# The low part of a weight piece in two halves in the delta-rule sections of a two-block transformer kernel

## The chip, the cores and the metric

The kernel runs on one core of one Trainium2 chip. The metric is device time in microseconds; lower is better. Before the change it is 1813.97 us, the median of three runs (1813.86, 1813.97 and 1814.95).

## The reference, cut to what matters

Two blocks of two layers each, on 256 tokens of width 1024, in float32. All weights are float32 and every projection is a dense product of the 256 rows with a weight matrix. In the second block a layer computes, among others, a gated delta rule over 8 heads:

```python
proj = h @ w_in                       # many sections of 1024 columns
(dn_q, dn_k, dn_v, dn_z, dn_b, dn_a, sw_q, sw_k, sw_v, gate_a, gate_b) = split(proj)
L = where(strict, einsum('id,jd->ij', k * beta, k) * decay, 0)
u = triangular_solve(L, v * beta)     # per head and chunk: (I + L)^-1
w = triangular_solve(L, k * beta * exp(g))
# then a scan over the chunks with a 128x128 state for each head
y_a = deltanet(...) @ w_up_dn
y_b = window_attention(...) @ w_up_sw
mix = (sigmoid(gate_a) * y_a + sigmoid(gate_b) * y_b) @ w_o
```

The triangular solves are done as an explicit inverse by doubling: seven levels, each a pair of small products that depend on the level before.

## The kernel before, in words

**Dense products.** Each float32 product is made of three products in the fast float32r format: the weight is cut into a high part `hi` and a remainder `lo`, the activations into `xh` and `xl`, and TensorE adds `xh*hi`, `xh*lo` and `xl*hi` (lines 400, 401 and 402, in `multiply`). A weight unit of 128 x 2048 values comes by one DMA from SyncE's queue into one of 4 buffers `raw` (`load_unit`). It is worked in two *pieces* of 128 x 1024. For each piece ScalarE copies `raw` to `hi` (line 372, `split_hi`, a ring of 6) and VectorE subtracts `raw - hi` into `lo` (line 382, `split_lo`, a ring of 5). A piece holds two row blocks of the weight (`kk` = 0 in the left 512 columns, 1 in the right 512), and TensorE does 12 matmuls of 128x512 on it: two row blocks by two token blocks by three terms. There are 504 pieces; 496 are 128x1024 and 8 are 128x544. TensorE waits on the semaphore `lo_ready` once for each call of `multiply`, for the whole piece. VectorE makes `lo` three pieces ahead of TensorE (`LO_LEAD`).

**The order of the work** is a list of steps written out by hand (`plan_one`, `plan_two`). Each engine runs through the same list and does its own share of each step, in order. `("piece", g)` is a piece of dense work. Between the pieces stand small steps: attention, transposes (`turn`), the delta rule. What an engine does at a step waits on semaphores of the engines that feed it, and everything behind it on that engine waits too.

**The delta-rule sections.** In each layer of the second block, the sections `gb`, `ga`, `zz` and `us` (32 pieces) are run with `halves=True`: TensorE does the first row block of a piece at `("piece", g, "half")`, then one slot of small steps, then the second row block at `("more", g)`, then another slot. So there are 64 slots. An even slot stands behind a first half, an odd one behind a second half:

```python
self.steps.append(("piece", g, "half"))
if between: self.steps.extend(between.pop(0))
self.steps.append(("more", g))
```

VectorE calls `split_lo` at `piece` for a whole piece of 128x1024 and does nothing for the dense work at `more`.

The delta rule works on four pairs of heads, `g` = 0 to 3. For each pair the steps `rows`, `betas`, `gram`, `gram_q`, `mask`/`join` and `inverse` prepare the matrices, then the levels follow, alternately `level_y` in an even slot and `level_t` in an odd slot. These are the lines that the prediction speaks of:

- L1601, TensorE at `level_y`: waits for the `inverse` of the level before and for a mask from POOL (L2214). L1617 and L1620, TensorE at `level_t`; L2111, VectorE at `level_t`: subtracts the result, which the next L1601 waits for.
- L1581, TensorE at `inverse` (an odd slot): waits for VectorE's L2105, which waits for POOL's mask L2205 and stands in VectorE's order behind `gram_q` (L2099, four instructions, the even slot before) for pairs 1 to 3. For pair 0 `gram` is in slot 3 (L2090), `gram_q` in slot 4 (L2099), and `inverse` in slot 7.
- L1983, VectorE at `squares_turn` (an odd slot, in pair 0's levels): copies 16 sums, from which POOL makes a reciprocal root (L924, L930). POOL's next mask (L2214) stands behind that. The convolution of `dv` (L1934, L1936, eight instructions) is VectorE's work of the even slot before.
- L1952 and L2122 are further VectorE steps in odd slots (a transposed copy, and the state of the delta rule).

Of the kernel before, what the change touches and what calls it, by code (L numbers as in the profile page):

```python
# [17 lines left out]
F32 = mybir.dt.float32  # L18
F32R = mybir.dt.float32r
I32 = mybir.dt.int32  # L20
ALU = mybir.AluOpType
# [16 lines left out]
RAW = 4  # L38
HI_RING = 6
LO_RING = 5  # L40
LEAD = 4
LO_LEAD = 3
# [225 lines left out]
class Core:  # L268
# [74 lines left out]
    def load_unit(self, sp, u):  # L343

        job, n, layer = self.units[u]
        if u >= RAW:
            sp.wait_ge(self.lo_ready, 2 * (u - RAW) + 2)
        slot, k = u % RAW, job.unit
        r0 = (job.row + n * k) * P
        src = self.ins[job.weight][layer, r0:r0 + k * P, job.col:job.col + job.cols].rearrange("(k p) c -> p k c", p=P)  # L350
        dst = self.raw[slot][:, 0:k * job.cols].rearrange("p (k c) -> p k c", k=k)
        if u == 0:
            sp.dma_start(dst[:, 0:k // 2, :], src[:, 0:k // 2, :]).then_inc(self.first_loaded, 16)
            dst, src = dst[:, k // 2:, :], src[:, k // 2:, :]
        sp.dma_start(dst, src).then_inc(self.unit_loaded[slot], 16)
# [16 lines left out]
            act.activation(self.hi[g % HI_RING][:, 0:w], src, ACT.Copy).then_inc(self.hi_ready, 1)  # L372
            self.hi_at = g + 1

    def split_lo(self, dve, upto):

        for g in range(self.lo_at, min(upto, len(self.pieces))):
            src, w = self.piece_raw(g)
            dve.wait_ge(self.hi_ready, g + 1)
            if g >= LO_RING:  # L380
                dve.wait_ge(self.pieces_used, g - LO_RING + 1)
            dve.tensor_tensor(self.lo[g % LO_RING][:, 0:w], src, self.hi[g % HI_RING][:, 0:w].bitcast(F32),  # L382
                              ALU.subtract).then_inc(self.lo_ready, 1)
            self.lo_at = g + 1

    def multiply(self, pe, g, rows=(0, 1), blocks=(0, 1)):


        job, n = self.pieces[g]
        pe.wait_ge(self.lo_ready, g + 1)  # L390
        k, c, slot = job.unit // 2, job.cols, g
        xh, xl = self.xh[job.xt], self.xl[job.xt]
        for kk in rows[:k]:
            row = job.xt_block + n * k + kk
            w = slice(kk * c, kk * c + c)
            for tb in blocks:
                out, t = self.bank[job.banks[tb]][:, 0:c], slice(tb * P, tb * P + P)
                first = job.start and n == 0 and kk == 0
                last = job.stop and n == job.pieces - 1 and kk == k - 1
                pe.matmul(out, xh[:, row, t], self.hi[slot % HI_RING][:, w], start=first, stop=False)  # L400
                pe.matmul(out, xh[:, row, t], self.lo[slot % LO_RING][:, w], start=False, stop=False)  # L401
                mm = pe.matmul(out, xl[:, row, t], self.hi[slot % HI_RING][:, w], start=False, stop=last)  # L402
        if rows[-1] >= k - 1 and blocks[-1] == TB - 1:
            mm.then_inc(self.pieces_used, 1)
        return mm
# [888 lines left out]
def block_two(nc, core, s, plans, ins):  # L1294
# [61 lines left out]
    parts = [(0, slice(0, P), own), (1, slice(P, 3 * P), both)]  # L1356
# [496 lines left out]
    def _(dve):  # L1853
        for plan in plans:
            layer, base = plan.layer, plan.base
            for what in plan.all_steps(s):
                kind, arg = what[0], what[1] if len(what) > 1 else None
                if kind in ("piece", "second"):
                    core.split_lo(dve, base + arg + LO_LEAD + 1)
                if kind == "first":  # L1860
                    core.split_lo(dve, base + min(arg + LO_LEAD + 1, what[2] + LO_RING))
                if kind == "x_final":
# [9 lines left out]
                if kind == "post_y":  # L1872
                    c, tb = what[2:]
                    cols = slice(c * CH, c * CH + CH)
# [13 lines left out]
                if kind == "turn_rows":  # L1888
                    tb, half = what[2:]
                    for j in range(4):  # L1890
                        n = 4 * half + j
# [8 lines left out]
                if kind == "turn":  # L1900
                    f = what[2]
                    bank = B[core.turn_bank[s.stage, arg, f]][:, :].rearrange("p (j t) -> p j t", j=2)
                    if is_cut(arg):
                        if arg[0] == "f":
                            k = 4 * (int(arg[1:]) % 2) + 2 * f
# [6 lines left out]
                        if arg == "yd":  # L1912
                            for j in range(2):
                                n = 2 * f + j
# [7 lines left out]
                    elif arg in conv_out:  # L1922
# [3 lines left out]
                        for j in (3, 2, 1, 0):  # L1926
                            if j < 3:
                                dve.wait_ge(*at("taps", (arg, f, j + 1)))
                            for n in range(2):
                                w = t.cols_all[:, layer, tap(j, first + 2 * f + n):tap(j, first + 2 * f + n) + 1]  # L1930
# [64 lines left out]
                if kind == "evac":  # L1995
                    job, name = plan.by_name[arg], arg[:2]
                    c = int(arg[-1])
                    cols = slice(c * CH, c * CH + CH)
# [107 lines left out]
                if kind == "level_t":  # L2106
                    g, l = arg, what[2]
# [199 lines left out]
```

## Time and profile before

| what | value |
|---|---|
| median of three runs | 1813.97 us |
| profiled execution, its own time | 1814.69 us |
| its span | 1812.9 us |
| TensorE busy | 1764.5 us, 97% |
| VectorE busy | 1148.3 us, 63% |
| ScalarE busy | 911.5 us, 50% |
| GpSimd (POOL) busy | 212.2 us, 12% |
| `lo` pieces (L382) | 504, 605.6 us in all |
| granted TensorE clock | 0.996 of full |

Times are of one profiled execution. The engines are called PE (TensorE), PEld (its weight loads), DVE (VectorE), ACT (ScalarE), POOL (GpSimd) and SP (SyncE). A matmul's record starts when it is issued and overlaps the next one, so the distance from start to start is what one costs. The same holds for short distances on DVE: an instruction may start a little before the one ahead of it has ended. "Idle before" is the time for which the engine had nothing running, and the arrow names what ended it; an engine with no idle time shown went on without a break.

### The profile page before, as it was taken

To read this page: it belongs to the slowest core of one execution; us is meant where nothing else is said; L and a number is where in the kernel's file an instruction comes from. 1 tells how busy PE (TensorE), PEld (TensorE's weight loads), DVE (VectorE), ACT (ScalarE), POOL (GpSimd) and SP (SyncE) were. 2 spreads that over 40 slices of the span, in tenths; PEclk is the share of its full clock that TensorE was granted. 3 is DMA by queue.
4 is the path that set the end of the run, shared out by engine and by line. 5 is a ranking of instruction groups with operands and counts; after the bars stand their busy time and mean duration, and the time that the engine had idled before them with its cause. 6 is when DMAs were issued, how large, how long until landed. Compare 5 with 4: busy or idle time off the path is not lost.

```text
span 1812.9 us, 27874 instructions
## 1 busy us (share of the span) xinstructions
PE 1764.5 (97%) x10637; PEld 1441.4 (80%) x10637; DVE 1148.3 (63%) x2136; ACT 911.5 (50%) x1646; POOL 212.2 (12%) x354
## 2 busy tenths in 40 slices
PE   9999999999999999999999999999999899999998
PEld 7878888887887788777787778888877787778887
DVE  5656667765666676687555675556587655675554
ACT  5355474543545646575444454446576334455443
POOL 2203000031030000301102000000301211100000
PEclk9999999999999999999999999999999999999999
DMA  8544445554444455432222555554533222445552
GB/s 302 170 136 142 159 140 166 186 178 171 140 140 159 137 176 193 162 117 94 75 89 81 174 163 187 186 186 147 199 120 101 70 90 71 163 159 176 184 185 87
DMA packets 137131, 270.07 MB, mean 149 GB/s; under 512 B 5548, under 2 KB 8744, under 8 KB 137000
## 3 DMA queue, kind: packets, MB, share of 16 engines
q1 hardware_dynamic: 134928, 265.44, 43.9%
q10 hardware_dynamic: 2072, 2.86, 0.5%
q8 instruction: 86, 1.41, 0.3%
q14 instruction: 45, 0.37, 0.1%
HBM read 267.23 MB, written 1.05 MB: 148 GB/s over the span
## 4 chain that ended last, share of the span: by engine, by line
PE 86%; DVE 6%; ACT 3%; POOL 3%; issue 2%; DMA 0%; ACTq 0%; DVEq 0%; POOLq 0%
PE bank L400 23%; PE bank L402 23%; PE bank L401 22%; PE bank L424 4%; PE bank L1601 1%; DVE buf L1936 1%; PE bank L1617 1%; DVE lo L382 1%; PE bank L1620 1%; POOL scratch L944 1%; POOL small L930 1%; PE bank L586 1%; PE bank L1572 1%; ACT hi L372 1%; DVE buf L1934 0%
## 5 line engine op out<-in xcount | busy, mean ns | idle before, releaser
L400 PE MATMUL bank<-hi,xh 128*128 128x512 f32 (+1 forms) x2016 | 816.8, 405 | 6.4 <-issue 2.9
L402 PE MATMUL bank<-hi,xl 128*128 128x512 f32 (+1 forms) x2016 | 787.0, 390 | 0.0
L401 PE MATMUL bank<-lo,xh 128*128 128x512 f32 (+1 forms) x2016 | 784.6, 389 | 0.0
L382 DVE TENSOR_TENSOR lo<-raw,hi 128x1024 fp32r<-128x1024 f32 (+1 forms) x504 | 605.6, 1220 | 52.8 <-PE bank L402 39.4
L372 ACT ACTIVATE hi<-raw 128x1024 fp32r<-128x1024 f32 (+1 forms) x504 | 519.5, 1048 | 208.2 <-PE bank L402 207.7
L400 PEld LDWEIGHTS bank<-hi,xh 128*128 128x128 f32 x2016 | 379.8, 188 | 86.9 <-issue 14.8
L402 PEld LDWEIGHTS bank<-hi,xl 128*128 128x128 f32 x2016 | 379.1, 188 | 81.7
L401 PEld LDWEIGHTS bank<-lo,xh 128*128 128x128 f32 x2016 | 380.5, 189 | 67.8
L424 PE MATMUL bank<-square,buf 128*128 128x128 f32 x584 | 88.9, 276 | 4.5 <-POOL buf L949 2.5
L424 PEld LDWEIGHTS bank<-square,buf 128*128 128x128 f32 x584 | 70.6, 141 | 21.8 <-issue 5.8
L1907 DVE TENSOR_TENSOR xl<-bank,xh 128x512 fp32r<-128x512 f32 x32 | 22.1, 692 | 90.6 <-ACT xh L1730 90.6
L1833 ACT ACTIVATE scratch<-bank 128x256 f32<-128x256 f32 (+1 forms) x48 | 18.4, 383 | 118.4 <-PE bank L1601 102.0
L488 POOL TENSOR_SCALAR small<-small 128x1 f32<-128x1 f32 (+1 forms) x13 | 4.7, 361 | 585.5 <-ACT scratch L481 585.4
L916 DVE CUSTOM_DVE_ANT_0 scratch<-bank,masks 128x128 f32<-128x128 f32 (+1 forms) x128 | 39.3, 354 | 47.6 <-PE bank L578 24.4
L1730 ACT ACTIVATE xh<-bank 128x512 fp32r<-128x512 f32 x32 | 19.2, 599 | 95.0 <-PE bank L424 95.0
L1936 DVE SCALAR_TENSOR_TENSOR buf<-bank,small,buf 128x255 f32<-128x255 f32 (+1 forms) x144 | 62.7, 477 | 2.5
L779 DVE TENSOR_SCALAR buf<-bank,small 128x512 f32<-128x512 f32 x48 | 33.8, 746 | 46.4 <-PE bank L402 46.4
L695 ACT ACTIVATE scratch<-scratch,small 128x128 f32<-128x128 f32 x64 | 28.6, 448 | 57.8 <-DVE small L916 57.8
L1802 ACT ACTIVATE scratch<-scratch,small 128x128 f32<-128x128 f32 x64 | 28.5, 447 | 34.6 <-DVE small L916 34.0
L2214 POOL TENSOR_TENSOR scratch<-scratch,narrow 128x256 f32<-128x256 f32 x40 | 31.6, 793 | 116.6 <-PE bank L1601 90.6
L2053 DVE SCALAR_TENSOR_TENSOR buf<-bank,small,buf 128x512 f32<-128x512 f32 x32 | 22.6, 747 | 28.7 <-ACT buf L1793 28.7
L763 DVE COPY buf<-bank 128x512 f32<-128x512 f32 x32 | 22.1, 690 | 29.2 <-PE bank L424 29.2
(295 smaller groups left out, 1711.7 us busy)
## 6 DMA issues: line engine op xcount, KB each, us to landing
raw<-in_w_in SPq DMA_DIRECT2D x135, 1024.0 KB, 5.1
raw<-in_w_ff SPq DMA_DIRECT2D x64, 1024.0 KB, 5.3
raw<-in_w_proj_a SPq DMA_DIRECT2D x8, 1024.0 KB, 5.1
raw<-in_w_proj_b SPq DMA_DIRECT2D x8, 1024.0 KB, 5.1
raw<-in_w_out SPq DMA_DIRECT2D x8, 1024.0 KB, 5.3
raw<-in_w_up_sw SPq DMA_DIRECT2D x8, 1024.0 KB, 5.0
raw<-in_w_up_dn SPq DMA_DIRECT2D x8, 1024.0 KB, 5.0
raw<-in_w_o SPq DMA_DIRECT2D x8, 1024.0 KB, 5.1
```

What stands on the lines that cost most here:

```text
L372: act.activation(self.hi[g % HI_RING][:, 0:w], src, ACT.Copy).then_inc(self.hi_ready, 1)
L382: dve.tensor_tensor(self.lo[g % LO_RING][:, 0:w], src, self.hi[g % HI_RING][:, 0:w].bitcast(F32), ALU.subtract).then_inc(self.lo_ready, 1)
L400: pe.matmul(out, xh[:, row, t], self.hi[slot % HI_RING][:, w], start=first, stop=False)
L401: pe.matmul(out, xh[:, row, t], self.lo[slot % LO_RING][:, w], start=False, stop=False)
L402: mm = pe.matmul(out, xl[:, row, t], self.hi[slot % HI_RING][:, w], start=False, stop=last)
L424: mm = pe.transpose(bank[:, (j * TB + tb) * P:(j * TB + tb + 1) * P], src[:, tb, c:c + P], core.ident)
L695: ins = act.activation(prob[h % 2][:, 0, cols], masked[:, h % 2, cols], ACT.Exp, scale=-1.0, bias=t.negmax[:, h % 2, tb:tb + 1], accum_out ...
L779: ins = dve.tensor_scalar(role[name][:, tb, cols], B[job.banks[tb]][:, :], t.r[:, s.stage, tb:tb + 1], None, ALU.mult)
L916: ins = dve.tensor_tensor_reduce(masked[:, cols], bank[:, cols], core.masks[:, which, keys], -SCALE, -NEG if negsink is None else negsink, ...
L1802: act.activation(prob[h % 2][:, cols], masked[h % 2][:, cols], ACT.Exp, scale=-1.0, bias=t1.negmax[:, h % 2, tb:tb + 1], accum_out=t1.tota ...
L1936: ins_ = dve.scalar_tensor_tensor(y, x, w, y, ALU.mult, ALU.add)
L2214: pool.tensor_tensor(lm[l % 2], diag[arg % 2], bcast(level_mask(l), 1, 4), ALU.mult)\
```

## The change

`split_lo` counts in half pieces. At `("piece", g, "half")` VectorE computes only the left 512 columns of the piece three ahead, and the right 512 at `("more", g)`, at the head of that step. Each half raises `lo_ready` by 1. Everywhere else a piece is computed whole, as before, by one instruction that raises `lo_ready` by 2. `multiply` waits for `lo_ready` in front of each row block, at `2g + 1 + kk`, so a whole piece has two waits in front of its products where it had one; SyncE's waits count in fours instead of twos. The 64 pieces of the delta-rule sections (32 in each of two layers) become 128 subtractions of 128x512. `LO_LEAD`, the rings and all other steps stay.

```diff
--- before.py
+++ after.py
@@ -344,7 +344,7 @@
 
         job, n, layer = self.units[u]
         if u >= RAW:
-            sp.wait_ge(self.lo_ready, 2 * (u - RAW) + 2)
+            sp.wait_ge(self.lo_ready, 4 * (u - RAW) + 4)
         slot, k = u % RAW, job.unit
         r0 = (job.row + n * k) * P
         src = self.ins[job.weight][layer, r0:r0 + k * P, job.col:job.col + job.cols].rearrange("(k p) c -> p k c", p=P)
@@ -372,25 +372,29 @@
             act.activation(self.hi[g % HI_RING][:, 0:w], src, ACT.Copy).then_inc(self.hi_ready, 1)
             self.hi_at = g + 1
 
-    def split_lo(self, dve, upto):
-
-        for g in range(self.lo_at, min(upto, len(self.pieces))):
+    def split_lo(self, dve, upto, half=False):
+
+        upto = min(upto, len(self.pieces))
+        while self.lo_at < (2 * upto - 1 if half else 2 * upto):
+            g, n = self.lo_at // 2, self.lo_at % 2
             src, w = self.piece_raw(g)
             dve.wait_ge(self.hi_ready, g + 1)
             if g >= LO_RING:
                 dve.wait_ge(self.pieces_used, g - LO_RING + 1)
-            dve.tensor_tensor(self.lo[g % LO_RING][:, 0:w], src, self.hi[g % HI_RING][:, 0:w].bitcast(F32),
-                              ALU.subtract).then_inc(self.lo_ready, 1)
-            self.lo_at = g + 1
+            parts = 1 if n or (half and g == upto - 1) else 2
+            cols = slice(n * w // 2, (n + parts) * w // 2)
+            dve.tensor_tensor(self.lo[g % LO_RING][:, cols], src[:, cols], self.hi[g % HI_RING][:, cols].bitcast(F32),
+                              ALU.subtract).then_inc(self.lo_ready, parts)
+            self.lo_at += parts
 
     def multiply(self, pe, g, rows=(0, 1), blocks=(0, 1)):
 
 
         job, n = self.pieces[g]
-        pe.wait_ge(self.lo_ready, g + 1)
         k, c, slot = job.unit // 2, job.cols, g
         xh, xl = self.xh[job.xt], self.xl[job.xt]
         for kk in rows[:k]:
+            pe.wait_ge(self.lo_ready, 2 * g + 1 + kk if k == 2 else 2 * g + 2)
             row = job.xt_block + n * k + kk
             w = slice(kk * c, kk * c + c)
             for tb in blocks:
@@ -1855,8 +1859,8 @@
             layer, base = plan.layer, plan.base
             for what in plan.all_steps(s):
                 kind, arg = what[0], what[1] if len(what) > 1 else None
-                if kind in ("piece", "second"):
-                    core.split_lo(dve, base + arg + LO_LEAD + 1)
+                if kind in ("piece", "more", "second"):
+                    core.split_lo(dve, base + arg + LO_LEAD + 1, what[-1] == "half")
                 if kind == "first":
                     core.split_lo(dve, base + min(arg + LO_LEAD + 1, what[2] + LO_RING))
                 if kind == "x_final":
```

## Rows read from the trace of the kernel before

**Rows 1.** The page: busy time by engine, and the chain that ended last.
```profile
PE 1764.5 (97%) x10637; PEld 1441.4 (80%) x10637; DVE 1148.3 (63%) x2136; ACT 911.5 (50%) x1646; POOL 212.2 (12%) x354
...
PE 86%; DVE 6%; ACT 3%; POOL 3%; issue 2%; DMA 0%; ACTq 0%; DVEq 0%; POOLq 0%
```

**Rows 2.** Windows over the two delta-rule stretches: start:end length, busy time (instructions), clock, DMA.
```profile
822.00:1015.00 193.00, 181.50 (x1819) 147.48 (x1820) 119.06 (x242) 85.61 (x154) 27.75 (x39) 0.98 0.28 92
1378.00:1572.00 194.00, 182.02 (x1822) 147.84 (x1822) 118.50 (x241) 85.50 (x155) 28.81 (x38) 0.98 0.28 92
```

**Rows 3.** Waits of TensorE, first stretch: us in total, times, longest.
```profile
PE bank L1601 <- POOL scratch L2214: 3.4, 1, 3.4
PE bank L1581 <- DVE buf L2105: 2.2, 2, 1.6
...
PE bank L1581 <- DVE scratch L2105: 1.2, 2, 0.6
```

**Rows 4.** Waits of TensorE, second stretch.
```profile
PE bank L1601 <- POOL scratch L2214: 4.5, 1, 4.5
```

**Rows 5.** Window of dense products without a break: ten pieces and three transposes.
```profile
361.47:388.71 27.24, 27.24 (x123) 22.43 (x121) 15.84 (x16) 13.80 (x18) 10.76 (x14) 1.00 0.59 203
```

**Rows 6.** Timeline, DVE pitch: start, length, engine, line, shapes, count [idle before <-releaser].
```profile
853.34 0.68 DVE L2111 TENSOR_TENSOR buf<-buf,bank 128x512 f32<-128x512 f32 x1
...
853.93 1.22 DVE L382 TENSOR_TENSOR lo<-raw,hi 128x1024 fp32r<-128x1024 f32 x1
853.98 0.40 PE L400 MATMUL bank<-hi,xh 128*128 128x512 f32 x1
...
854.21 0.39 PE L401 MATMUL bank<-lo,xh 128*128 128x512 f32 x1
...
854.76 0.68 PE L1601 MATMUL bank<-buf,scratch 64*64 64x64 f32 x16
```

**Rows 7.** Timeline, inverse step of the first pair of heads.
```profile
839.13 1.21 DVE L382 TENSOR_TENSOR lo<-raw,hi 128x1024 fp32r<-128x1024 f32 x1
...
840.27 1.12 DVE L2090 SCALAR_TENSOR_TENSOR buf<-bank,small,buf 128x128 f32<-128x128 f32 x4
...
843.96 1.35 DVE L382 TENSOR_TENSOR lo<-raw,hi 128x1024 fp32r<-128x1024 f32 x1
...
845.23 0.94 DVE L2105 TENSOR_TENSOR buf<-narrow,buf 128x256 f32<-128x256 f32 x1
...
846.32 0.68 PE L1581 MATMUL bank<-narrow,buf 64*64 64x64 f32 x16 [1.59 <-DVE buf L2105]
```

**Rows 8.** Timeline of VectorE around the 128x544 piece.
```profile
712.58 2.99 DVE L382 TENSOR_TENSOR lo<-raw,hi 128x544 fp32r<-128x544 f32 x3
```

**Rows 9.** Timeline, inverse step of a pair of heads in the first stretch.
```profile
881.22 1.13 DVE L2099 SCALAR_TENSOR_TENSOR scratch<-bank,small,scratch 128x128 f32<-128x128 f32 x4 [1.08 <-PE bank L1572]
...
881.33 0.73 POOL L2205 TENSOR_TENSOR scratch<-scratch,narrow 128x256 f32<-128x256 f32 x1 [15.46 <-ACT scratch L1823]
...
882.26 0.77 DVE L2105 TENSOR_TENSOR scratch<-narrow,scratch 128x256 f32<-128x256 f32 x1
...
883.18 0.68 PE L1581 MATMUL bank<-narrow,scratch 64*64 64x64 f32 x16 [0.62 <-DVE scratch L2105]
```

**Rows 10.** Timeline of VectorE, a step in an odd slot that follows idle time.
```profile
895.15 0.42 DVE L2122 COPY scratch<-bank 128x256 f32<-128x256 f32 x1 [3.56 <-PE bank L1641]
```

**Rows 11.** Timeline, rsqrt chain of the first stretch.
```profile
859.58 0.16 DVE L1983 COPY small<-bank 128x16 f32<-128x16 f32 x1
...
860.23 2.91 POOL L930 TENSOR_TENSOR small<-small 128x16 f32<-128x16 f32 x1
...
863.93 0.97 PE L1601 MATMUL bank<-buf,scratch 64*64 64x64 f32 x13 [3.41 <-POOL scratch L2214]
```

**Rows 12.** Windows at the lower clock, one in each stretch.
```profile
862.97:869.79 6.82, 5.86 (x33) 5.18 (x34) 3.49 (x8) 1.67 (x2) 2.27 (x4) 0.50 0.41 147
1419.35:1426.15 6.80, 5.74 (x32) 5.07 (x33) 3.43 (x8) 1.67 (x2) 2.37 (x4) 0.50 0.29 114
```

## The prediction

> **What bounds the kernel now.** I read the page first. TensorE is busy for 97% of the span and carries 86% of the chain that ended last; VectorE is busy for 63% and carries 6% [rows 1]. So the time is TensorE's own work plus its stops, and an edit on VectorE is worth what it does to those stops. Next the windows over the two delta-rule stretches, the only place where `lo` is split: TensorE stands still for 193.00 - 181.50 = 11.5 us in the first and 194.00 - 182.02 = 12.0 us in the second [rows 2]. That bounds any gain. The list of waits says who ends the stops: in the first stretch POOL's mask once for 3.4 us, and VectorE's L2105 four times for 2.2 + 1.2 = 3.4 us [rows 3]; the second has the same entries for L2105, and 4.5 us on POOL [rows 4]. None is ended by `lo` (L382): the dense products don't wait for the subtraction here, it is three pieces ahead. What L382 can do is stand in front of other VectorE work. So I went through VectorE's timeline slot by slot and asked at each of the 128 slots what is ready when `lo` stands ahead of it.
>
> **The change part by part.**
>
> *Waits of TensorE.* Outside the split sections (440 pieces) a second wait per piece is added, already satisfied, since both counts come with one update. The nearest rows are dense stretches that already hold one satisfied wait a piece. In one, 123 matmuls start within 27.24 us; three are transposes at the edge, the other 120 are ten pieces [rows 5]. 27.24 / 120 = 0.227 us each, waits included, and inside a row block, where there is no wait, two matmuls start at 853.98 and 854.21, 0.23 apart [rows 6]. I take 0. Upper end: an estimate from the weight loads' spare time in that window, 27.24 - 22.43 = 4.8 us over 121 loads, 0.04 us each [rows 5]; if a wait takes as much and is not covered, 440 x 0.04 = 18 us. Below zero it can't go, as nothing is taken away. The increment by 2 instead of 1 is not in the trace; it rides on the same instruction, and what would have to wait for it is three pieces ahead: 0, with the same cover.
>
> *SyncE's queue.* A unit's load now waits for the second half of its old tenant's second piece, half a piece later in the split sections. The loads are four units ahead and no stop of TensorE ends on a DMA there [rows 3, 4]. 0.
>
> *Price of a half on VectorE.* A 128x512 float32 subtraction, L2111, starts at 853.34 and lets the next start at 853.93: 0.59 us; it runs for 0.68 but overlaps [rows 6]. Three pieces, a 128x544 ahead of two of 128x1024, take 2.99 us; less 1.14 for a whole piece with a successor (839.13 to 840.27, rows 7) and 1.22 for the last, the 544 costs 0.63 [rows 8]. Both say 0.60 for 512 columns. So splitting costs 2 x 0.60 - 1.14 = 0.06 us a piece, 64 x 0.06 = 4 us of VectorE time, in an engine with 37% to spare. The lower end of a half is half of 1.14 = 0.57, the upper its record length, 0.68.
>
> *Where it lands.* That is the point of the change. In even slots VectorE's work used to have 1.14 us of `lo` ahead of it and now has 0.60; in odd slots it had none and now has 0.60.
> A gain needs an even slot whose VectorE work starts late because of `lo` and ends in a TensorE stop. I found none: `gram_q` (L2099) waits 1.08 us for TensorE's L1572 with VectorE idle [rows 9], and the other even-slot work of the levels likewise waits for a matmul. 0.
> In odd slots the half is free where VectorE was idle ahead of the work: L2122 after 3.56 us [rows 10], others after less, where the slack ahead of TensorE covers the rest. Most odd slots are of this kind. Where `level_t` directly follows a convolution (L2111 at 853.34), it moves to 853.94 and ends at 854.62; the L1601 behind it started at 854.76, and where TensorE stands waiting it starts 0.15 after VectorE's record ends (883.03 to 883.18, rows 9), so 854.77: free by a hair [rows 6].
> It is not free where VectorE is unbroken ahead of something that TensorE stands waiting for. Three kinds:
>
> 1. `inverse` of pairs 1 to 3. L2099 starts at 881.22, its fourth part ends as L2105 starts at 882.26 without a break; POOL's mask is ready at 881.33 + 0.73 = 882.06, so VectorE's order sets the start, and TensorE takes up L1581 at 883.18, after 0.62 us idle [rows 9]. The slot of `inverse` is odd, so the second half comes exactly between L2099 and L2105: +0.60 us on TensorE. 3 pairs x 2 layers x 0.60 = 3.6 us.
> 2. `inverse` of pair 0. Ahead of L2105 at 845.23 VectorE is unbroken from 839.13 [rows 7]. It is in slot 7; the halves for slots 2 to 7 add up to the whole pieces that were there (three; the group leaves one out), so only the splitting counts: 3 x 0.06 = 0.18, less what the rearranged waits take up; I take 0.15, 0.3 us in two layers.
> 3. The rsqrt chain. L1983 at 859.58 stands unbroken behind a convolution; POOL's L930 follows at 860.23 for 2.91 us, the mask, and L1601 at last at 863.93, TensorE having been idle for 3.41 us [rows 11]. The half goes ahead of L1983: +0.60, 1.2 us in two layers.
>
> *The clock.* After each of these two long stops the granted clock is 0.50, the 1.2 GHz level, for 6.8 us, and TensorE works 5.86 and 5.74 us of it [rows 12]. A stop 0.6 longer has two readings: if the low stretch ends at the same moment, 0.6 us less is worked at half speed and 0.3 comes back; if its end moves with the return of the work, nothing does. Stops of 3.4 and 4.5 us leave nearly the same time worked at the low level, so I take the second: +0.60 each, with 0.30 as the lower end. The other stops grow from at most 1.6 [rows 3] to about 1.8 us, and today's of 1.6 are not followed by a fall (clock 0.98 over the stretch, which the one 6.8 us stretch explains: 1 - 0.5 x 6.8 / 193 = 0.982 [rows 2]).
>
> *Sum.* 3.6 + 0.3 + 1.2 = 5.1 us. The ends: with 0.57 a half and 0.30 for the chain 2 x (3 x 0.57 + 0.30) = 4.0; with 0.68 and 0.15 a split piece 2 x (4 x 0.68 + 3 x 0.15) = 6.3. On the profiled execution's own time of 1814.69 (span 1812.9 + 1.8) that is 1819.8; that execution is 0.72 above the median, and the two layers' L930 chains differ by 1.1 us in it (3.4 against 4.5 idle), about the spread of the three runs, so I add to the median: 1813.97 + 5.1 = **1819.1 us**.
>
> A rule that speaks against the change: the Trainium skill, "VectorE: DVE Perf Modes", section "The TRN2 errata — SBUF-src ops pay a fixed extra latency per instruction", says that many small operations pay a fixed cost that one large one pays once, and gives (N + 151) / 0.96 ns for a float32 tensor_tensor: 691 ns for 512 columns and 1224 for 1024, so 157 ns for each split. By it the sum is an estimated 2 x (4 x 0.691 + 3 x 0.157) = 6.5 us. The record lengths agree (0.68 for a 512-column operation, 1.22 for a piece, rows 6); the starts say that 0.08 us of it is overlapped by the neighbour.
>
> **The rivals.**
> - *No overlap between the halves and their neighbours.* Each costs its record length: 6.3 us, 1820.3. For it: a half must wait for semaphores that the row's neighbours did not. Against: whole pieces carry the same waits and overlap.
> - *Not slower: the clock does not fall.* Place: the two long stops. The fall there costs (5.86 + 5.74) x 0.5 = 5.8 us today [rows 12]. If the fall depends on how the stops lie in time and not on their length alone, a shift of 0.2 us or more could lose one or both: 1819.1 - 2.9 = 1816.2, or 1813.3 with both. It decides at whether the idle 3.4 us is still answered. Against: two stops of different length were both answered, and they only get longer.
> - *The clock stays low longer.* The opposite: if the low stretch lasts half as long again, 3.4 us more at half speed is 1.7 a layer, 1822.5.
> - *Partly absorbed.* If L2105 is really set by POOL's mask plus a delay (0.20 us from 882.06 to 882.26, rows 9) that goes on beside the half, some of the six stops don't grow: with half of them 5.1 - 1.8 = 3.3, 1817.3. For it: the 0.20 us. Against: the half starts only after L2099 in either case.
> - *The new waits are not covered*: up to 18 us, 1836. Against: rows 5. It would show in both blocks. The Trainium skill ("Trainium Kernel Development and Optimization", section "Key Constraints") says that compute semaphores increment by 1; no row here has a 2, and what it would cost no page says. If such updates were slow, it would be this rival's time or part of it.
> - *Faster*: a gain in an even slot that I missed, at most the other stops, say 1811.
>
> **How the numbers follow.** Forecast 0.50 (own range 1818.0 to 1820.3, the ends of the sum); no overlap 0.08; clock does not fall 0.07; clock low longer 0.08; partly absorbed 0.18; waits uncovered 0.03; faster by something missed 0.06. This kernel's runs tell 0.2% (3.6 us) from no change. Slower by more, above 1817.6: 0.50 + 0.08 + 0.08 + 0.03 = 0.69, less 0.03 for a forecast that comes out a little short: 0.66. Within: 0.18 + 0.06 + 0.03 = 0.27. Faster: 0.07. The range leaves out the uncovered waits, the faster case, part of the lost fall and the upper part of the longer low stretch: 1814.8 to 1821.8.
>
> **What would show it.** In the trace after: 128 subtractions of 128x512 into `lo` in the two stretches, about 0.69 us long; the record ahead of L2105 in pairs 1 to 3 is `lo`, and TensorE's idle time ahead of L1581 is about 1.2 instead of 0.62; the idle time ahead of the L1601 behind POOL is 4.0 and about 5.1 (or either 1.1 more or less, as L930 varies); the dense window still gives 0.227 a matmul; all else equal. I am wrong if TensorE's idle time in the stretches does not grow by 2 to 3 us in each, if the low-clock stretches vanish or lengthen, or if time moves in the first block.

## The result: slower, by more than forecast

The changed kernel takes 1824.62 us (median of five, 1821.90 to 1825.13) against 1813.97 before on the same chip. The two medians differ by 10.7 us. The ratio on record is smaller, 1.0046 with a 95% interval of 1.0034 to 1.0058, that is +8.3 us (6.2 to 10.5); with the average of the five runs, 1823.9, it fits an average of 1815.6 for the kernel before, which is what the larger sets of its runs beside the experiments give (medians 1815.42 to 1816.00). The 1813.97 that the forecast was added to is thus about 1.5 us low. Measured again, the change took 1822.45 us, a ratio of 1.0039 (1.0026 to 1.0053), +7.1 us. Forecast were +5.1 us and a range up to 1821.8: the side was right, the size too small, and the time outside the range.

The profiled execution took 1824.98 us with a span of 1823.2. VectorE has its 64 more instructions (2136 before, 2200 now) and 6.6 us more of busy time; TensorE's busy time grew by 4.0 us with the same 10637 matmuls [rows 1]; the granted clock fell from 0.996 to 0.992, and the windows below show where.

```profile
PE 1768.5 (97%) x10637; PEld 1444.1 (79%) x10637; DVE 1154.9 (63%) x2200; ACT 911.9 (50%) x1646; POOL 210.2 (12%) x354
```

The windows over the same work as [rows 2], moved to where it now lies. TensorE stands still for 15.1 and 14.6 us, 3.6 and 2.6 more than before, and works 1.2 and 0.9 us longer; the clock is 0.97 instead of 0.98.

```profile
823.85:1021.65 197.80, 182.69 (x1819) 148.21 (x1820) 120.82 (x272) 85.69 (x154) 28.43 (x39) 0.97 0.27 86
1384.65:1582.20 197.55, 182.96 (x1821) 148.40 (x1822) 120.35 (x271) 85.60 (x155) 28.39 (x38) 0.97 0.26 86
```

The lines behind line 375 have moved by 4: L382 is now L386, L1581 is L1585, L1601 is L1605, L1983 is L1987, L2099 is L2103, L2105 is L2109, L2111 is L2115, L2214 is L2218. TensorE's waits in the first stretch [rows 3]: the inverse steps went from 2.2 + 1.2 to 3.4 + 2.4 us.

```profile
PE bank L1605 <- POOL scratch L2218: 4.6, 1, 4.6
PE bank L1585 <- DVE buf L2109: 3.4, 2, 2.2
PE bank L1585 <- DVE scratch L2109: 2.4, 2, 1.2
```

**Where the time went.** Both traces hold the same 10637 matmuls in the same order. So I took, for each, its start after less its start before, and noted where that difference steps. Almost all of it is flat.

| place | first layer | second layer | forecast, each |
|---|---|---|---|
| stop ahead of `inverse`, pair 0 | +0.61 | +0.61 | +0.15 |
| low clock after that stop | +1.51 | +1.48 | 0 |
| stop behind the rsqrt chain | +1.18 | +0.06 | +0.60 |
| low clock after that stop | -0.32 | -0.45 | 0 |
| stops ahead of `inverse`, pairs 1 to 3 | +1.80 | +1.79 | +1.80 |
| start of the kernel | +0.56 | | 0 |
| low clock at 799 us, ahead of the sections | +1.23 | | 0 |
| all else | +0.1 | | 0 |

They sum to 10.2 of the 10.3 us by which the span grew. The second trace of the changed kernel has +0.60/+0.61 and +1.49/+1.46 at pair 0, 1.82 and 1.79 for pairs 1 to 3, +1.17 with -0.47 and +0.07 with -0.53 at the rsqrt chain, but nothing at 799 us, and stops 1.1 us less at 745: its span is 7.8 us over before.

*Pairs 1 to 3.* The inverse step that answers to [rows 9]. A 128x512 subtraction now stands between L2103 and L2109, and TensorE's idle time is 1.22 us instead of 0.62, to the hundredth as forecast. It comes about a little differently: the half takes 1.04 us, not 0.68, as POOL's mask runs beside it, and the inverse behind it takes 0.41 instead of 0.77.

```profile
886.04 1.13 DVE L2103 SCALAR_TENSOR_TENSOR scratch<-bank,small,scratch 128x128 f32<-128x128 f32 x4 [1.60 <-PE bank L1576]
...
886.85 0.73 POOL L2218 TENSOR_TENSOR scratch<-scratch,narrow 128x256 f32<-128x256 f32 x1
...
887.08 1.04 DVE L386 TENSOR_TENSOR lo<-raw,hi 128x512 fp32r<-128x512 f32 x1
...
888.05 0.41 DVE L2109 TENSOR_TENSOR scratch<-narrow,scratch 128x256 f32<-128x256 f32 x1
...
888.61 0.68 PE L1585 MATMUL bank<-narrow,scratch 64*64 64x64 f32 x16 [1.22 <-DVE scratch L2109]
```

*Pair 0*, [rows 7]: between the end of L2103 and L2109 are three halves, 2.95 us in all, while POOL's two masks take 2.40.

```profile
844.31 1.13 DVE L2103 SCALAR_TENSOR_TENSOR buf<-bank,small,buf 128x128 f32<-128x128 f32 x4
...
845.36 2.95 DVE L386 TENSOR_TENSOR lo<-raw,hi 128x512 fp32r<-128x512 f32 x3
845.36 2.40 POOL L2218 TENSOR_TENSOR scratch<-scratch,narrow 128x256 f32<-128x256 f32 x2
...
848.23 0.41 DVE L2109 TENSOR_TENSOR buf<-narrow,buf 128x256 f32<-128x256 f32 x1
...
848.79 0.68 PE L1585 MATMUL bank<-narrow,buf 64*64 64x64 f32 x16 [2.20 <-DVE buf L2109]
```

The line view of L386 over those three: shortest, median and longest time in ns. The first takes 0.68, the other two 1.2 us each, double of what 512 columns cost elsewhere.

```profile
L386 DVE TENSOR_TENSOR lo<-raw,hi x3: 681/1206/1224, 845.4 to 847.1; 128x512 fp32r<-128x512 f32 x3
```

*The rsqrt chain*, [rows 11]. The half stands ahead of L1987 as forecast and moves it by 0.60 us. But POOL's L930 (now L934) changed too: it takes 3.48 us in both layers, where it took 2.91 and 4.01 before. So TensorE's stop grew by 0.60 + 0.57 = 1.17 us in the first layer and by 0.60 - 0.53 = 0.07 in the second.

```profile
863.57 0.68 DVE L386 TENSOR_TENSOR lo<-raw,hi 128x512 fp32r<-128x512 f32 x1
...
864.17 0.17 DVE L1987 COPY small<-bank 128x16 f32<-128x16 f32 x1
...
864.82 3.48 POOL L934 TENSOR_TENSOR small<-small 128x16 f32<-128x16 f32 x1
864.85 0.69 DVE L386 TENSOR_TENSOR lo<-raw,hi 128x512 fp32r<-128x512 f32 x1
...
869.09 1.12 PE L1605 MATMUL bank<-buf,scratch 64*64 64x64 f32 x16 [4.59 <-POOL scratch L2218]
```

Before, a whole subtraction started 0.02 us behind L930 in both layers. In the second layer L930 then took 4.01 us; in the first it took 2.91, and the subtraction 1.27.

```profile
860.25 1.27 DVE L382 TENSOR_TENSOR lo<-raw,hi 128x1024 fp32r<-128x1024 f32 x1
...
1415.61 4.01 POOL L930 TENSOR_TENSOR small<-small 128x16 f32<-128x16 f32 x1
1415.63 1.22 DVE L382 TENSOR_TENSOR lo<-raw,hi 128x1024 fp32r<-128x1024 f32 x1
```

The thirteen traces on record (two layers each) say what sets the length of L930 at this step:

| VectorE's subtraction that starts 0.02 us behind L930 | L930 | cases |
|---|---|---|
| none (third and seventh experiment, and the version that beats both) | 2.91 us | 6 of 6 |
| 128x512 (the change twice, both halves at the old place, the change without the slots, with masks late, with pair 0 as before) | 3.47 to 3.48 us | 12 of 12 |
| 128x1024 (before, the signals alone, before with masks late, only pair 0 changed) | 4.01 us | 7 of 8 |
| the same | 2.91 us | 1 of 8: first layer of the trace of before |

L930 is longer by 0.57 and 1.10 us, about what 512 and 1024 columns of subtraction take from start to start. A subtraction that starts 0.49 us into L930, in the first block, leaves it at 2.93 us. So the trace of before that all of this is compared with holds the one unusual case: against 4.01 us, the change adds 0.07 us at this chain in each layer, and not 0.60.

*The clock.* Windows over all low stretches of the changed kernel between start and end: 50% each. The ones at 867 and 1427 answer to [rows 12]; those at 850 and 1410, behind pair 0's stop, and at 799 are new. In the one at 867 TensorE works for 5.21 us instead of 5.86, in the one at 1427 for 4.76 instead of 5.74: half of the difference, 0.33 and 0.49 us, is what came back there.

```profile
799.21:802.62 3.41, 3.41 (x12) 2.73 (x11) 2.16 (x7) 3.41 (x8) 0.55 (x3) 0.50 0.22 31
850.41:853.82 3.41, 3.41 (x25) 2.52 (x24) 0.19 (x1) 0.81 (x2) 0.00 (x0) 0.50 0.01 2
867.47:874.30 6.83, 5.21 (x30) 4.53 (x31) 2.90 (x7) 1.67 (x2) 2.93 (x4) 0.50 0.00 0
1410.20:1413.60 3.40, 3.40 (x24) 2.42 (x23) 0.00 (x0) 1.26 (x2) 0.00 (x0) 0.50 0.13 50
1427.27:1434.08 6.81, 4.76 (x28) 4.09 (x29) 2.49 (x6) 1.67 (x2) 3.36 (x4) 0.50 0.00 0
```

*The dense window* that answers to [rows 5], now with two waits for each piece: unchanged.

```profile
362.02:389.26 27.24, 27.24 (x123) 22.45 (x121) 15.84 (x16) 13.83 (x18) 10.87 (x14) 1.00 0.60 204
```

### The profile page after: what moved, and what is told of

Same layout as the page of the kernel before. It is cut to its first block, busy times and chain, and to the rows that moved or that the text cites. A ratio compares the mean times of both kernels' runs of the same rounds, so it can differ in the third digit from the quotient of the medians.

```text
span 1823.2 us, 28007 instructions
## 1 busy us (share of the span) xinstructions
PE 1768.5 (97%) x10637; PEld 1444.1 (79%) x10637; DVE 1154.9 (63%) x2200; ACT 911.9 (50%) x1646; POOL 210.2 (12%) x354
## 4 chain that ended last, share of the span: by engine, by line
PE 54%; DVE 5%; POOL 3%; ACT 2%; issue 2%; DVEq 0%; POOLq 0%; ACTq 0%
PE bank L404 14%; PE bank L406 14%; PE bank L405 14%; PE bank L428 2%; PE bank L1605 1%; DVE lo L386 1%; DVE buf L1940 1%; PE bank L1621 1%; PE bank L1624 1%; POOL scratch L948 1%; POOL small L934 1%; PE bank L1576 1%; DVE buf L1938 0%; PE bank L1564 0%; PE bank L1653 0%
## 5 line engine op out<-in xcount | busy, mean ns | idle before, releaser
L386 DVE TENSOR_TENSOR lo<-raw,hi 128x1024 fp32r<-128x1024 f32 (+1 forms) x568 | 618.6, 1108 | 54.9 <-PE bank L406 40.4
L2218 POOL TENSOR_TENSOR scratch<-scratch,narrow 128x256 f32<-128x256 f32 x40 | 31.0, 778 | 120.0 <-PE bank L1605 90.5
```

The source lines that it names most:

```text
L386: dve.tensor_tensor(self.lo[g % LO_RING][:, cols], src[:, cols], self.hi[g % HI_RING][:, cols].bitcast(F32), ALU.subtract).then_inc(self.l ...
L2218: pool.tensor_tensor(lm[l % 2], diag[arg % 2], bcast(level_mask(l), 1, 4), ALU.mult)\
```

## The experiments

All ratios are to runs of the kernel before that ran beside them. "Low" is a stretch of the clock at 1.2 GHz. Where the edit moves lines, the rows keep the names of buffers and shapes; the kernels made from the changed one have its numbers.

**The signals alone.**

```diff
-                    core.split_lo(dve, base + arg + LO_LEAD + 1, what[-1] == "half")
+                    core.split_lo(dve, base + arg + LO_LEAD + 1)
```

> Only the signals of the change: every piece is still one subtraction of 128x1024 at its old place, but it raises lo_ready by 2, and TensorE waits in front of each row block. Theory (order on VectorE): nothing, 1814 to 1816 us, with TensorE's stops ahead of the inverse steps of pairs 1 to 3 at 0.62 us as before. Rival (waits and increments by 2 cost): a difference of 2 us or more, spread evenly over the kernel, also over the first block.

1816.22 against 1816.00 us, ratio 1.0000 (0.9991 to 1.0008). Its trace is 1.6 us longer than that of before, and all of that comes in the first 14 us of the kernel, ahead of the sections. Behind them the stop of the first rsqrt chain is 4.52 us instead of 3.41 (L930 took 4.01), and a shorter low stretch there takes that back. Two waits a piece and increments by 2 cost nothing that can be measured: that rival falls.

**Both halves at the old place.**

```diff
-                if kind in ("piece", "more", "second"):
+                if kind in ("piece", "second"):
                     core.split_lo(dve, base + arg + LO_LEAD + 1, what[-1] == "half")
+                    if what[-1] == "half":
+                        core.split_lo(dve, base + arg + LO_LEAD + 1)
```

> The change with both halves issued at the first half of the dense products, so two subtractions of 128x512 stand where the whole one stood. Theory (order on VectorE): stops of pairs 1 to 3 stay at 0.62 us idle and the one behind the rsqrt chain at 3.4 to 4.5; pair 0's stop grows by up to 0.3, as POOL's masks and VectorE's two-input operations take turns there; in all 1814 to 1817. Rival (splitting itself costs): all stops where VectorE is unbroken grow by 0.06 to 0.16, and 64 splits add 4 to 10 us: 1818 to 1824.

1815.65 against 1816.00, ratio 1.0001 (0.9992 to 1.0010). Splitting costs nothing that can be measured, though a gain of 1.1 us may hide a loss of that size: with two halves behind it L934 takes 3.48 us in both layers, 0.53 less than behind a whole piece, so the second half adds nothing to it.

```profile
862.25 3.48 POOL L934 TENSOR_TENSOR small<-small 128x16 f32<-128x16 f32 x1
862.27 1.30 DVE L386 TENSOR_TENSOR lo<-raw,hi 128x512 fp32r<-128x512 f32 x2
```

The timeline at pair 0: two halves in 1.82 us, idle 1.67 instead of 1.59, less growth than I had allowed.

```profile
844.55 1.82 DVE L386 TENSOR_TENSOR lo<-raw,hi 128x512 fp32r<-128x512 f32 x2
...
846.86 0.68 PE L1585 MATMUL bank<-narrow,buf 64*64 64x64 f32 x16 [1.67 <-DVE buf L2111]
```

And at pair 1, where the stop is 0.62 us, as before:

```profile
885.45 0.68 PE L1585 MATMUL bank<-narrow,scratch 64*64 64x64 f32 x16 [0.62 <-DVE scratch L2111]
```

**The whole piece moved, nothing split** (on the kernel before).

```diff
-                if kind in ("piece", "second"):
+                if kind in ("piece", "more", "second") and what[-1] != "half":
```

> No split and no new signals: the kernel before with the whole subtraction moved from the first half of the dense products to the second, so that 1.14 us stand ahead of the odd slots. Theory (order on VectorE): each of the six inverse stops of pairs 1 to 3 grows by 1.14 us (idle 0.62 to 1.76), the two stops behind the rsqrt chain by 1.14, pair 0's by 1 to 2, and the clock falls after pair 0's and perhaps after others: 9.1 + 3 + 3 = 15 us, 1829 (1824 to 1835). Rival (the split and its signals cost, not the place): 1814 to 1816.

1826.19 against 1816.00, ratio 1.0055 (1.0042 to 1.0067): +10 us where I had said 8 to 19. The place alone does it. The inverse steps of pairs 1 to 3 grow by 1.13 to 1.14 us each, 6.8 in all:

```profile
882.90 1.13 DVE L2099 SCALAR_TENSOR_TENSOR scratch<-bank,small,scratch 128x128 f32<-128x128 f32 x4 [2.11 <-PE bank L1572]
...
883.94 1.58 DVE L382 TENSOR_TENSOR lo<-raw,hi 128x1024 fp32r<-128x1024 f32 x1
...
886.00 0.68 PE L1581 MATMUL bank<-narrow,scratch 64*64 64x64 f32 x16 [1.75 <-DVE scratch L2105]
```

Two `level_t` slots in each layer, too, are no longer free with 1.14 us in front (0.46 to 1.12 us idle where there was none). I had expected 15 us. Pair 0 grew by only 0.40, to 2.01 us idle, not by 1 to 2, with no low stretch behind it; and the rsqrt stops are 4.56 us in both layers, where 1.14 more than 4.51 was expected: nothing runs beside L930 there, and it takes 2.91 us.

```profile
862.32 2.91 POOL L930 TENSOR_TENSOR small<-small 128x16 f32<-128x16 f32 x1
```

**The change without the slots that TensorE waits for.**

```diff
-                    self.steps.append(("piece", g, "half"))
+                    around = {what[0] for what in sum(between[:2], [])}
+                    early = bool(around & {"mask", "inverse", "squares_turn"})
+                    self.steps.append(("piece", g, *["early"] * early, "half"))
...
-                    core.split_lo(dve, base + arg + LO_LEAD + 1, what[-1] == "half")
+                    core.split_lo(dve, base + arg + LO_LEAD + 1, what[-1] == "half" and "early" not in what)
```

> The change, but with a whole subtraction at its old place in the slots around mask, inverse and squares_turn; the other halves stay as in the change. Theory (order on VectorE): all of the loss is at those places, so 1814 to 1816, no stop of TensorE longer than before by over 0.1 us and no new low stretch of the clock in the delta-rule sections. Rival (halves in any odd slot cost something): 1817 or more.

1813.80 against 1816.00, ratio 0.9993 (0.9984 to 1.0001). All of the loss is at those slots; the halves in the others are free. The stops at the inverses are as before. Those behind the rsqrt chain are 3.99 and 3.98 us, since a half and not a whole piece runs beside L930 (3.48 us); that is 0.53 a layer less than beside a whole one, and the ratio allows for it. The other steps in the difference to before are low stretches behind the stop of 1.48 us idle that the attention has at 798 and 1354 us, +1.2 each, and shorter ones behind the rsqrt chain, -1.1 and -1.0.

**POOL's masks of pair 0 later, in the changed kernel.**

```diff
                     elif arg:
                         pool.wait_ge(*at("level_y", (arg - 1, LEVELS + l - 3)))
+                    else:
+                        pool.wait_ge(*at("inverse", (0, 0)))
```

> The change, and POOL makes the first two level masks of pair 0 (L2214 of the kernel before) only when VectorE's first inverse is done, so that no POOL work runs beside the three halves ahead of it. Theory (POOL's and VectorE's two-input operations take turns): the two long halves there shrink from 1.22 to about 0.68 us, TensorE's idle time ahead of the inverse of pair 0 from 2.2 to 1.1 to 1.3 us, and no low stretch of the clock follows it; 2 x (1.0 + 1.5) = 5 us less than the change: 1817 to 1821. Rival (the halves are long for another reason, or the fall of the clock does not hang on that stop): idle time stays at 2.2 us, and the time at that of the change.

1817.71 against 1815.42, ratio 1.0012 (1.0003 to 1.0020), so 2.2 us over before instead of 7 or 8. The three halves now take 1.88 us in a row, about 0.6 each, TensorE's idle time is 1.13, and no low stretch follows in either layer. The time was at the lower end of what I expected, since the stop is now shorter even than before. One stop is new: 0.52 us idle at the L1605 of the first `level_t` slot behind the rsqrt chain, in the second layer. In the change the low stretch ahead of that place is 6.83 us long instead of 3.41, so TensorE comes later and is not idle there.

```profile
843.67 1.88 DVE L386 TENSOR_TENSOR lo<-raw,hi 128x512 fp32r<-128x512 f32 x3
...
845.47 0.42 DVE L2109 TENSOR_TENSOR buf<-narrow,buf 128x256 f32<-128x256 f32 x1
...
845.97 1.11 POOL L2220 TENSOR_TENSOR scratch<-scratch,narrow 128x256 f32<-128x256 f32 x1 [2.25 <-DVE buf L2109]
...
846.04 0.68 PE L1585 MATMUL bank<-narrow,buf 64*64 64x64 f32 x16 [1.13 <-DVE buf L2109]
```

**The same in the kernel before.**

> The same delay of POOL's two masks in the kernel before. Theory (taking turns): the whole subtraction ahead of the inverse of pair 0 takes 1.22 instead of 1.35 us, the inverse itself about 0.4 instead of 0.94, TensorE's idle time there falls from 1.59 to about 0.9 us: 1.3 us less in two layers, 1812 to 1815. Rival (masks needed earlier): TensorE's next L1601 starts late and takes the gain back.

1814.67 against 1815.42, ratio 0.9995 (0.9987 to 1.0004): no difference that can be told, though the stop shrank as expected, from 1.59 to 0.93 us, in both layers. This pair of experiments divides what the change does at pair 0. With POOL's masks out of the way the change adds 1.13 - 0.93 = 0.20 us, which is the splitting; with the masks there it adds 0.61. So about 0.41 us of it comes from POOL.

```profile
844.41 1.22 DVE L382 TENSOR_TENSOR lo<-raw,hi 128x1024 fp32r<-128x1024 f32 x1
...
845.54 0.42 DVE L2105 TENSOR_TENSOR buf<-narrow,buf 128x256 f32<-128x256 f32 x1
...
846.11 0.68 PE L1581 MATMUL bank<-narrow,buf 64*64 64x64 f32 x16 [0.93 <-DVE buf L2105]
```

For comparison the row of the kernel before that [rows 7] leaves out, POOL's two masks, which ran beside one whole piece there:

```profile
843.49 2.40 POOL L2214 TENSOR_TENSOR scratch<-scratch,narrow 128x256 f32<-128x256 f32 x2
```

**The rsqrt chain ahead of the convolution** (on the kernel before).

```diff
-(0, "y2"): [("turn", "dv", 2)], (0, "t2"): [("squares_turn", "dq")],
+(0, "y2"): [("squares_turn", "dq"), ("turn", "dv", 2)],
```

> The kernel before with the step squares_turn of dq one slot earlier and ahead of the convolution, so that POOL's reciprocal root starts some 3.5 us earlier. Theory (VectorE's order and POOL's chain make the two long stops, and these make the low clock behind them): the stops of 3.4 and 4.5 us shrink to under 1 us each and the low stretches behind them go, 6 to 8 us plus up to 5.8: 1801 to 1808. Rival (something else is late next, or the clock falls anyway): less than 6 us gained.

1804.79 against 1815.42, ratio 0.9938 (0.9926 to 0.9951). The stops of 3.41 and 4.51 us are 0.32 and as small in the second layer, and both low stretches are gone: 5.8 and 6.8 us gained at these places, less 0.5 each at a later `level_t`. L1983 starts at 856.32 instead of 859.58:

```profile
856.32 0.17 DVE L1983 COPY small<-bank 128x16 f32<-128x16 f32 x1 [0.93 <-PE bank L1509]
...
856.99 2.92 POOL L930 TENSOR_TENSOR small<-small 128x16 f32<-128x16 f32 x1
...
857.67 2.69 DVE L1936 SCALAR_TENSOR_TENSOR buf<-bank,small,buf 128x255 f32<-128x255 f32 x6
...
860.27 0.68 DVE L2111 TENSOR_TENSOR buf<-buf,bank 128x512 f32<-128x512 f32 x1
...
861.10 0.59 PE L1601 MATMUL bank<-buf,scratch 64*64 64x64 f32 x13 [0.32 <-DVE buf L2111]
```

L930 took 2.91 us in both layers here, beside the convolution. That is part of the gain of the new order: no subtraction of `lo` starts with it any more, which is worth 1.1 us wherever it took 4.01.

**The change a second time.**

> The changed kernel again, to see what of its 10.3 us of longer span comes back in a second trace. Theory: the six inverse stops +0.6 each, pair 0 +0.6 twice, rsqrt chain +0.6 twice up to POOL's own variation of 1.1: 6 us that are always there. Open: whether the low stretch of the clock after pair 0's stop (1.5 us a layer) comes in both layers again; if it does it belongs to the change, if not it is chance. The low stretches at the start and at 799 us (0.6 and 1.3 us) should not come back if they are chance.

1822.45 against 1815.42. What came back and what not is told with the table above: the low stretches behind pair 0 did, that at 799 us did not; that at the start did, but six of the eleven other traces have one there too, two of them of kernels without the change, so it is not the change's.

**Pair 0 as before, the rest changed.** The edit is that of the fourth experiment with `early` for `("mask", 0)` and `("inverse", 0)` alone.

> The change, but with whole subtractions at their old place in the four slots around mask and inverse of pair 0. Theory (the fall of the clock after pair 0's stop belongs to the longer stop, 2.20 us idle instead of 1.59): the stops of pairs 1 to 3 and of the rsqrt chain grow as in the change, 3.6 + 1.2 us, pair 0's stop is 1.6 us as before and no low stretch follows it: 4 to 5.5 us over before, 1818 to 1820. Rival (the low stretch there is chance or comes from the rest of the change): it shows in this kernel too, and the loss is 7 us or more.

1818.38 against 1815.58, ratio 1.0016 (1.0007 to 1.0025): +2.9 us (1.3 to 4.5), less than the expected 4 to 5.5. The inverse steps of pairs 1 to 3 grew by 0.60 to 0.61 each as expected. The rsqrt stops are 4.59 and 4.58 us, only 0.07 above the usual 4.51, not the 0.6 that I had counted; low stretches there of 3.41 us instead of 6.83 save 1.2 a layer against the trace of before, and the `level_t` behind them now costs 0.3 and 0.6. Pair 0's stop is 1.60 us, with no low stretch behind it; the first stretch's waits hold 1.6 for pair 0 and 1.2 for each of the others (its L1587 is L1581 of before, its L2111 is L2105):

```profile
PE bank L1587 <- DVE buf L2111: 2.8, 2, 1.6
PE bank L1587 <- DVE scratch L2111: 2.4, 2, 1.2
```

**Only pair 0 changed**, the opposite choice of `early`.

> The change in those four slots of pair 0 alone (two split pieces in each layer), all other pieces whole at their old place. Theory: pair 0's stop 2.2 us idle and a low stretch behind it in both layers: 2 x (0.6 + 1.5) = 4.2 us, less 0.3 to 0.4 a layer if the low stretch of the rsqrt chain shifts. Rival: 1.2 us and no low stretch.

1819.07 against 1815.58, ratio 1.0019 (1.0010 to 1.0028): +3.5 us. The stop is 2.14 and 2.13 us idle. In the first layer a low stretch follows, in the second none. Windows behind the two stops:

```profile
848.00:851.40 3.40, 3.40 (x18) 2.37 (x20) 0.28 (x1) 1.33 (x2) 0.00 (x0) 0.51 0.78 253
1406.00:1409.40 3.40, 3.40 (x30) 2.63 (x30) 0.88 (x3) 1.61 (x3) 0.00 (x0) 1.00 0.81 269
```

**A version that beats both.** The seventh experiment, POOL's masks of pair 0 late, and the whole subtraction of slot 6 behind the inverse instead of ahead:

```diff
-                    self.steps.append(("piece", g, "half"))
+                    late = len(between) > 1 and ("inverse", 0) in between[1]
+                    self.steps.append(("piece", g, *["late"] * late, "half"))
...
+                if "late" in what:
+                    behind = base + arg + LO_LEAD + 1
-                if kind in ("piece", "second"):
+                elif kind in ("piece", "second"):
                     core.split_lo(dve, base + arg + LO_LEAD + 1)
...
                     dve.tensor_tensor(first, bcast(core.narrow[:, 0, :], 1, 4), first, ALU.subtract).then_inc(*up("inverse", (arg, 0)))
+                    if arg == 0:
+                        core.split_lo(dve, behind)
```

> The kernel before with squares_turn ahead of the convolution, POOL's first two masks of pair 0 behind the first inverse, and VectorE's whole subtraction of slot 6 behind that inverse instead of ahead of it. Theory: 11 us from the first edit as measured, and pair 0's stop of 1.59 us idle shrinks to under 0.3, 1.2 us in each layer: 1801 to 1804. Rival (the masks or the subtraction are late for the next step): no better than the first edit alone, 1804.8.

1801.04 against 1815.58, ratio 0.9923 (0.9911 to 0.9936), 14 us less than before and about 22 less than the change. Its L2102 is L2099 of before, 2108 is L2105 and 1582 is L1581. The inverse now follows L2102 directly, and TensorE's L1582 has no idle time ahead of it to show:

```profile
844.66 1.12 DVE L2102 SCALAR_TENSOR_TENSOR buf<-bank,small,buf 128x128 f32<-128x128 f32 x4
...
845.70 0.41 DVE L2108 TENSOR_TENSOR buf<-narrow,buf 128x256 f32<-128x256 f32 x1
...
846.40 0.68 PE L1582 MATMUL bank<-narrow,buf 64*64 64x64 f32 x16
```

## Why the prediction came out wrong

**Right.** The method, reading at each odd slot whether VectorE was idle, found the places that cost in the changed kernel: the fourth experiment, without them, is no slower than before. One more, a `level_t` behind the rsqrt chain, costs up to 0.6 us once the low stretch there is short. The price of 0.60 us for a half at pairs 1 to 3 was right to 0.02. The new waits, the increments by 2 and SyncE's queue cost nothing that can be measured. The "no overlap" rival and the rule of the Trainium skill on a fixed cost per operation ("VectorE: DVE Perf Modes", section "The TRN2 errata — SBUF-src ops pay a fixed extra latency per instruction") would both have charged 0.68 to 0.69 us for a half where 0.60 was measured; the length of its record, 0.68, does agree with that page.

**Wrong, first step: "`inverse` of pair 0 ... only the splitting counts: 3 x 0.06 = 0.18".** It was +0.60 to +0.61 in four stops. I added up VectorE's pieces as if each took its own time. The splitting was priced right: with POOL's masks late in both kernels, the stop grows by 0.20. The rest, 0.41, is POOL. Of the three halves two took 1.2 us beside POOL's masks, and about 0.60 each once the masks were made to wait. The times fit turn-taking: the two masks end at about 846.6 and 847.8 and the two long halves about 0.55 us behind each. Before, one whole piece and one mask stood ahead of L2105 to take turns; three halves let both masks in. The rows had said so: a piece of 1.35 us instead of 1.21 and an inverse of 0.94 instead of 0.77 [rows 7, 9]. The Trainium skill has it as well ("GPSIMD Engine Reference", section "1. Specifications"): the SBUF interfaces are shared with VectorE, with contention where its instruction has two SBUF inputs; `raw - hi` has two. That section gives no figure. That the turn lasts one instruction is my reading; L930 bears it out, which waits 0.57 us for a half, 1.10 for a whole piece, and again 0.57 where two halves follow each other.

**Wrong, second step: "The other stops grow from at most 1.6 [rows 3] to about 1.8 us, and today's of 1.6 are not followed by a fall".** They grew to 2.2, and the clock fell behind it: 1.5 us in each layer, the largest term that was missing. Here the traces together say more than one does. TensorE's idle time ahead of pair 0's inverse, and low stretches within 5 us behind it:

| idle time there | stops | followed by a fall |
|---|---|---|
| 0 to 1.13 us (masks late) | 6 | 0 |
| 1.59 to 1.60 | 10 | 0 |
| 1.66 to 1.67 | 2 | 1 |
| 2.00 to 2.01 | 2 | 0 |
| 2.13 to 2.21 | 6 | 5 |

So the fall belongs to the longer stop, but not with certainty. The attention's stop of 1.48 us was followed by one in 5 of 26 cases. The rival "clock low longer" had the sign and about the size (+1.7 a layer) but the wrong place: the stretches behind the rsqrt chain stayed 6.83 us long and gave back 0.3 to 0.5 each. That is not the half of a longer stop that my lower end allowed for, since the second layer's stop grew by 0.07 only; TensorE worked less time at the low clock.

**Wrong, third step, and hidden by luck: "The half goes ahead of L1983: +0.60", and "1.1 more or less, as L930 varies".** I took L930 for a wait of fixed length with chance on top. Its length follows the subtraction that starts with it, and the change itself replaced a whole piece by a half there. The +1.18 and +0.06 of the table sum to my 1.2 us only because the trace of before has the rare 2.91 us in its first layer. Against the usual 4.01 the term is 2 x 0.07 = 0.14.

With 0.6 for pair 0, 1.5 for the clock and -0.4 behind the rsqrt chain, the sum against the trace of before is 2 x (1.8 + 0.6 + 0.6 + 1.5 - 0.4) = 8.2 us; against an execution of before with 4.01 us in both layers it is 2 x (1.8 + 0.6 + 0.07 + 1.5 - 0.4) = 7.1. Measured were 8.3 and 7.1, and the intervals hold both. The first median of 1824.62 lies about 2 us above 1815.6 plus 7.1: its profiled execution has the low stretches at 799 us and at the start, 1.8 us, and kernels without the change have such stretches too. In the chances of the prediction the 0.06 of "faster by something missed" and the 0.07 of "clock does not fall" are interchanged between "within" and "faster".

What stays open is when the clock falls: 2.0 us idle did not do it in two cases, 2.13 to 2.14 did in one of two. Open is also why L930 escaped once in eight.

## What to carry to other kernels

Moving work on an engine with time to spare costs exactly where that engine runs without a break in front of something that the full engine waits for; read the idle time ahead of each step, not the engine's busy share. Look at what else runs at that moment: two-input subtractions on VectorE and masks on POOL slowed each other, so cutting VectorE's work into more operations can let more of POOL's in ahead of the result, and what an edit puts beside an instruction of POOL can change that one's length. A stop of TensorE has a price beyond its length once the clock falls behind it, and that makes the longest stops the first thing to mend: here one step moved ahead of a convolution gave 11 us, more than the whole change cost.

## What the hardware showed that I had not expected

- A 128x512 subtraction took 0.68 us alone and 1.04 to 1.22 beside POOL's 128x256 products; POOL's took 0.73 alone, up to 1.27 beside a half and 1.71 beside a whole piece.
- The clock fell to 1.2 GHz behind stops as short as 1.48 us in some executions; such a low stretch of 3.4 us cost 1.2 to 1.5 us. It may be a good part of the scatter between runs of one kernel; that is not shown.
- POOL's reciprocal root on 128x16 values (L930) took 2.91 us when no subtraction of `lo` started with it, 3.48 when one of 128x512 did, and 4.01 when one of 128x1024 did (7 of 8 cases), though its own record starts 0.02 us ahead of the subtraction's. An operation on 16 columns is longer by about the whole of the other.
